# Sixteen gate tiles computed in the front's seven-product pairs instead of in the mixer steps

## The reference, cut to what matters

```python
u = rms_norm(x, norm_mix_pre_w)
proj = u @ w_in
z, xbc, dt_raw, q, k, v, gate_ssd, gate_attn = _split(proj, IN_SIZES)
xbc = jax.nn.silu(causal_dwconv(xbc, ssd_conv_w, ssd_conv_b))
...
y = gated_group_rms_norm(y.reshape(b, s, SSD_D_INNER).astype(x.dtype), z, ssd_norm_w)
y_ssd = y @ ssd_w_out
q = apply_rope(q.reshape(b, s, ATTN_N_KV_HEADS, ATTN_REP, ATTN_HEAD_DIM), cos, sin)
...
y_attn = sliding_window_sink_attention(q, k, v, attn_sinks) @ attn_w_out
merged = jax.nn.sigmoid(gate_ssd) * y_ssd + jax.nn.sigmoid(gate_attn) * y_attn
```

## Time and profile before

| | us |
|---|---|
| median of 3 runs | 2077.04 (2076.82 to 2079.41) |
| the profiled execution, its own time | 2077.58 |
| its span, first to last instruction | 2075.9 |
| PE busy | 2012.1 (97%) |
| DVE busy | 1339.8 (65%) |
| ACT busy | 968.4 (47%) |
| POOL busy | 603.2 (29%) |
| mean granted clock of TensorE | 0.991 |

### The profile page before, as it was taken

The page is one execution under the profiler, slowest core; times in us unless marked ns, Lnnn a source line. Parts: engine busy times, 40 slices in busy tenths (PEclk is TensorE's granted clock), DMA queues, the critical chain, the costliest instruction groups (busy, mean ns, idle before and its releaser), DMA issues. The chain is left out here.

```text
span 2075.9 us, 27004 instructions
## 1 busy us (share of the span) xinstructions
PE 2012.1 (97%) x9612; PEld 1625.5 (78%) x9612; DVE 1339.8 (65%) x1812; ACT 968.4 (47%) x1815; POOL 603.2 (29%) x445
## 2 busy tenths in 40 slices
PE   6999999989999999999999999999999999999997
PEld 6777877867777777777678888888888888888886
DVE  6878787766666666666634445569877787753523
ACT  5633543535665565655633223335444444444432
POOL 6533234244444354444300000024222222100000
PEclk9999999999999999999999999999999999999999
DMA  4334244364443444433454333222212221455443
GB/s 157 91 112 142 92 134 151 100 203 139 129 139 120 139 143 129 139 109 113 151 200 167 124 145 142 105 80 82 91 66 86 91 89 62 165 175 184 121 147 91
DMA packets 168396, 262.00 MB, mean 126 GB/s; under 512 B 18656, under 2 KB 109152, under 8 KB 168288
## 3 DMA queue, kind: packets, MB, share of 16 engines
q1 hardware_dynamic: 129568, 208.15, 31.5%
q0 software_dynamic: 8368, 30.94, 4.4%
q10 hardware_dynamic: 30352, 21.50, 3.2%
HBM read 191.73 MB, written 63.57 MB: 123 GB/s over the span
## 5 line engine op out<-in xcount | busy, mean ns | idle before, releaser
L2792 DVE TENSOR_TENSOR lt_d_lo<-lt_w_raw,lt_d_hi 128x640 fp32r<-128x640 f32 (+1 forms) x62 | 55.3, 892 | 133.4 <-ACT lt_d_hi L2491 133.3
L1538 POOL TENSOR_TENSOR mx_seg<-mx_seg,mx_cbm 128x1024 f32<-128x1024 f32 x31 | 75.2, 2426 | 168.4 <-ACT mx_seg L1635 168.4
L162 PE MATMUL ps_zg<-u_hi,g_hi 128*128 128x512 f32 x256 | 109.8, 429 | 1.9 <-DVE g_lo L1212 1.9
L162 PE MATMUL ps_zg<-z_w,u_hi 128*128 128x512 f32 x256 | 103.9, 406 | 3.6 <-DVE z_w L1714 3.6
L2362 POOL TENSOR_TENSOR lt_t_f<-lt_w_raw 128x512 f32<-128x512 f32 x21 | 29.1, 1387 | 261.7 <-DVE lt_t_lo L2720 260.2
L2491 ACT ACTIVATE lt_d_hi<-lt_w_raw 128x640 fp32r<-128x640 f32 (+1 forms) x62 | 49.1, 792 | 118.6 <-PE lt_ps L164 102.9
L164 PE MATMUL ps_zg<-u_hi,g_lo 128*128 128x512 f32 x256 | 102.2, 399 | 0.0
L163 PE MATMUL ps_zg<-u_lo,g_hi 128*128 128x512 f32 x256 | 101.8, 398 | 0.0
L164 PE MATMUL ps_zg<-z_w,u_lo 128*128 128x512 f32 x256 | 100.3, 392 | 0.0
L163 PE MATMUL ps_zg<-z_w,u_hi 128*128 128x512 f32 x256 | 99.8, 390 | 0.0
L2449 ACT ACTIVATE lt_t_hi<-lt_t_f 128x512 fp32r<-128x512 f32 x84 | 52.4, 628 | 100.1 <-PE lt_ps L164 61.9
(11 more groups left out here) (553 smaller groups left out, 6612.1 us busy)
## 6 DMA issues: line engine op xcount, KB each, us to landing
lt_w_raw<-in_w_up SPq DMA_DIRECT2D x44, 512.0 KB, 4.5
work<-acs_s SPq DMA_DIRECT2D x32, 512.0 KB, 4.2
lt_sig<-gate_s SPq DMA_DIRECT2D x24, 512.0 KB, 3.5
lt_w_raw<-in_w_down SPq DMA_DIRECT2D x32, 384.0 KB, 3.2
ff_s<-lt_fo SPq DMA_DIRECT2D x21, 512.0 KB, 5.4
tok_s<-fr_xt SPq DMA_DIRECT2D x20, 512.0 KB, 3.2
lt_w_raw<-in_w_down SPq DMA_DIRECT2D x32, 320.0 KB, 3.0
g_raw<-in_w_gate SPq DMA_DIRECT2D x16, 512.0 KB, 6.7
```

What stands on the lines that cost most here:

```text
L162: pe.matmul(dst, s_hi, m_hi, start=first, stop=False, skip_group_check=onto)
L1538: pool.tensor_tensor(seg[:], (carry.a_row[:, 0] if opening else seg[:]), cbm[:].unsqueeze(1).to_broadcast([P, HPG, P]), ALU.mult).then_inc ...
L2792: dve.tensor_tensor(down_w(m)[1][:, 0:n], w_raw[:, m % 2, 0:n], down_w(m)[0][:, 0:n].bitcast(F32), ALU.subtract).then_inc(dw_lo_done, 1)
```

## The change

The gate product leaves the mixers. `ORDER` gets eight pairs of kind "g", spread among the others, and the front computes the 16 gate tiles as such pairs: seven block products each, two plain copies to `xc` on ACT and a store of each by SP (`store_gate`). The last pair is now a gate pair, so that the front no longer ends with a convolution and a silu. In the mixers the gate products, the splits of their weights (ACT, DVE), the copy of the result, its DMA and the loads of gate weights are gone. The weights of the attention's output, which used the gate's place, are loaded at c = 4 of the last group by SP. Both banks of `ps_zg` now hold z in turn. z of the next step is cut in two: k from 0 to 3 (`AHEAD = 4`) after the turned outputs, the rest where it stood; z of the next group's first step stays whole behind the diagonal products. The table work of the front (dt, sums) moves to the iterations after gate and rotary pairs. Slots 1 and 2 of PSUM change places.

In numbers of instructions PE loses 768 matmuls of the mixers and gains 672 in the front. ACT and DVE lose 16 splits of 1024 elements and ACT loses 32 copies; in the front they gain 56 splits each of 512 elements, ACT 8 copies of a partial product and 16 of tiles (128 by 1024), DVE 40 additions of 512 elements, and POOL 32 sums of weights.

The diff, cut to its core:

```diff
-ORDER = (("c", 0), ("c", 1), ("r", 0), ("c", 8), ("r", 4), ("c", 10), ("c", 2), ("c", 3), ("r", 1), ("c", 4), ("c", 9),
-         ("r", 2), ("c", 5), ("c", 6), ("c", 7), ("r", 3), ("c", 11))
+ORDER = (("c", 0), ("c", 1), ("g", 0), ("r", 0), ("c", 8), ("g", 1), ("r", 4), ("c", 10), ("g", 2), ("c", 2), ("c", 3),
+         ("r", 1), ("g", 3), ("c", 4), ("c", 9), ("r", 2), ("g", 4), ("c", 5), ("c", 6), ("g", 5), ("c", 7), ("g", 6),
+         ("c", 11), ("r", 3), ("g", 7))
...
+            def store_gate(n):
+                t = tiles[n]
+                sp.wait_ge(kept, t.kept_n + 1)
+                sem = carry.g_late if t.i == LAST else g_stored[t.j]
+                sp.dma_start(gate_s[t.f], xc[:, t.j]).then_inc(sem, 16)
...
             taken(2 * i)
             high_z(6)
             high_z(7)
-            act.wait_ge(carry.g_in[0], 16)
-            act.wait_ge(product_done, OPS * (i - 1) + 5)
-            act.activation(carry.g_hi[:, 0], carry.g_raw[:, 0], ACT.Copy).then_inc(carry.g_hi_done, 1)
             taken(2 * i + 1)
-            silu(2 * i)
-            silu(2 * i + 1)
...
-                if i == 2:
+                if i == 3:
                     table_dt_first()
-                if i == 4:
+                if i == 6:
                     table_dt_rest()
...
             last.then_inc(carry.z_done, 1)
-            pe.wait_ge(carry.g_lo_done, 1)
-            for k in range(4):
-                matmul3(pe, carry.ps[:, 1], carry.g_hi[:, 0, k], carry.g_lo[:, 0, k], u_hi[:, k, 0:HALF],
-                        u_lo[:, k, 0:HALF], k == 0, False)
+            for k in range(AHEAD):
+                matmul3(pe, carry.ps[:, 1], u_hi[:, k, P:2 * P], u_lo[:, k, P:2 * P], carry.z_hi[:, k], carry.z_lo[:, k],
+                        k == 0, False)
...
+            def z(g, c, ks):
+                n = NT * g + c
+                if ks[0] == 0 and n >= 2:
+                    pe.wait_ge(z_used, n - 1)
...
+                    def ahead(*ks):
+                        if c < NT - 1:
+                            z(g, c + 1, range(*ks))
+
                     if not opening:
-                        gate(g, c, range(0, 4), opening)
                         values(*before)
...
-                    gate(g, c, range(4, 6), opening)
...
                     if not opening:
                         turn_outputs(*before, first and c == 1)
-                    gate(g, c, range(6, KT), opening)
+                    if not opening:
+                        ahead(0, AHEAD)
...
-                    next_z(g, c, last_group, range(KT))
+                    ahead(AHEAD, KT)
+                    if c == NT - 1 and not last_group:
+                        z(g + 1, 0, range(KT))
```

More of the change, by code:

```diff
@@ L31 @@
 TH = NT // 2
+AHEAD = 4
 KH = KT // 2
@@ L407, in xc_free @@
             before = tiles[n - 2]
-            if not before.conv:
+            if before.rot:
                 eng.wait_ge(q_stored[before.j], 16 * (before.q_n + 1))
+            if before.gate:
+                eng.wait_ge(g_stored[before.j], 16 * (before.gate_n + 1))
             if before.turns:
@@ L419, in xt_free @@
                 return
-            before = next((t for t in reversed(tiles[:n]) if t.j == n % 2 and (t.turns or not t.conv)), None)
+            before = next((t for t in reversed(tiles[:n]) if t.j == n % 2 and (t.turns or t.rot)), None)
             if before.conv:
@@ L1457, in group @@
                 for c in range(NT):
-                    if c % 2 == 0:
-                        u = 4 * g + c // 2
-                        if not (last and c == NT - 2):
-                            src = A["w_attn_out"][0] if last and c == NT - 4 else A["w_gate"][u + 2]
-                            sp.wait_ge(g_lo_done, u + 1)
-                            sp.dma_start(g_raw[:, (c // 2) % 2], src).then_inc(g_in[(c // 2) % 2], 16)
+                    if last and c == NT - 4:
+                        for j in range(2):
+                            sp.dma_start(g_raw[:, j], A["w_attn_out"][j]).then_inc(out_in[j], 16)
                     if last and c == NT - 1:
@@ L1657, in group @@
                         split_o(0)
-                    if change:
-                        gate_tile(g, c, first)
                     if change:
@@ L1668, in group @@
                     ins.then_inc(exp_done, 1)
-                    if not change:
-                        gate_tile(g, c, first, ending)
-                    if last and c == NT - 3:
-                        act.wait_ge(g_lo_done, 2 * KT)
-                        act.dma_start(g_raw[:, 1], A["w_attn_out"][1]).then_inc(g_in[1], 16)
                     if not (last and c == NT - 1):
@@ L1705, in _ @@
             outputs(NG - 1, NT - 1, False, False)
-            for j in range(2):
-                act.wait_ge(g_stored[j], 16 * NG * NT // 2)
         @block.vector
```

187 lines of the change are left out of this document (69 added, 118 removed).

## The result

The changed kernel takes 2127.03 us (median of 4, 2126.54 to 2128.89) where the kernel before takes 2076.93: a ratio of 1.0242, 95% interval 1.0225 to 1.026, so 50 us slower. The forecast was 2111, the range 2090 to 2142. The profiled execution has a span of 2124.8 us for 2075.9 before, 48.9 us more.

What follows compares the result with a forecast made beforehand. The kernel was taken as bound by matmuls on PE, the changed mixers by latency over ACT and DVE. 152.3 - 12 - 96 - 10.5 = +33.8 us on 2077.58 gave 2111 us, range 2090 to 2142.

Steps and rivals of the forecast that it cites:

- Term 1: Front: eight added gate pairs of 19.04 us each cost PE +152.3 us; their work on other engines is covered.
- term 2: Front: about half of PE's stalls in the pairs go, -12 us (between -5 and -20).
- Term 3: Mixers' steps: the ACT and DVE chain sets them, 15.2 us a middle step; -96 us (between -85 and -106).
- Rival C: Mixers' steps: the clock falls once a step, +50 us, so about 2160 us; chance 0.06.
- Rival B: Mixers' steps stay bound by PE because the chain holds slack; 12.7 us a step, kernel 2034 us; chance 0.06.
- Term 4: Joint of front and mixers: earlier mixer start and lighter first step, together -10.5 us (between -7 and -13).
- rival D: Mixers: POOL's blocking or loads put a middle step at 16 to 16.5 us, +25 us, 2136 us; chance 0.10.

Runs made afterwards that it cites:

- e9_loads: The changed kernel with only SP's loads of the step after next issued some 4.5 us sooner: 2131.11 us.
- e5_tail: The changed kernel with the last 6 of a step's 24 z products behind its transposes of the scores: 2122.99 us.
- e3_mask_first: The changed kernel with DVE's mask and maximum ahead of its product with z in all steps but the last: 2121.15 us.
- e2_z_behind: The changed kernel with all of z behind the diagonal products in every step: 2264.90 us.
- e7_all: e6_mask_tail plus DVE's SBUF sum for y before its wait for the diagonal products, 6 next-group z products earlier at c = 7, ACT's output-weight splits later: 2087.38 us.
- e6_mask_tail: The changed kernel with the edits of e3_mask_first and e5_tail together: 2107.44 us.

## Why the prediction was right, and where its terms were off

**Term 1 and term 2, the front.** +152.3 - 12 = +140.3 was forecast, +141.3 came. The last product of the pairs ends at about 573.7 us for the 572 forecast. The waits fell by 9.2 us, from 17.8 to 8.6; the first one, 3.6 us, stayed as said. By an estimate from the granted clock, its lower level cost 6.8 us in the pairs before (0.57 over 99 to 107 us, 0.66 over 126 to 131 and 174 to 179) and costs 5.2 now (0.57 over 100 to 108 and over 240 to 244), 1.6 less. Together 10.8 us went where I took 12, and 152.3 - 10.8 = 141.5 is close to the measured 141.3. The pair's price of 19.04 us was right, and the run with two gate pairs confirms that nothing beside matmuls is paid.

**Term 3, the mixers.** -96 was forecast, -84.7 came, and this is where the forecast lost 11.3 of the 15 us that its sum is short. Middle steps (15.17 for 15.2), c = 0 (13.1 for 13.1), the waits for the copy (1.11 for 1.1) and the product with z (+6.77 for +6.78) came as worked out. The misses by step: c = 7 took 21.08, 19.89 and 21.01 for 18.3 each, +7.1 us in three; the last two 16.72 and 16.71 for 15.2 and 15.3, +2.9; c = 1 14.75 to 15.26 for 14.7, +1.3 in four, of which the late loads are the part that e9_loads takes away (14.75 in all four). That is the +11.3 between 472 and 483.2. The step of the working that failed is the one on c = 7. I noted that the whole z stays behind the diagonal products there, and counted the splits on DVE and POOL, but did not ask what then covers ACT's copy of the turned outputs, which I had found to be covered by little in a middle step. Before, all 24 gate matmuls of a step stood ahead of the product with the state, the last 6 of them right over this copy. With them gone and no z in their place it is a wait of 2.89 us, and the clock falls at its end. The run with the filler puts the step at 18.5, so 6.4 of the 7.1 us are this wait and its clock.

**Rival C** had 0.06. As told, a fall in every step, it did not come: the granted clock over the mixers is 0.96, and 1.00 in the middle steps. But its mechanism is what made c = 7 long, at 3.5 us a fall and not the 1.6 that I took from the front, and in the run with all of z behind it came in each step and cost more than the +50 I gave it: of the 140.0 us by which the mixers are longer there, the waits for ACT's copy make 83 at most (26 of 2.89 us and two of 3.83). In the middle steps an empty wait of 1.1 us was followed by no fall, and one of 2.89 us by a fall in most steps. The Trainium skill, page "TensorE: Matmul & The Clock Gate", section "A second HAM failure mode: psum-queue depth-cycling", lets short idle gaps between groups of matmuls make the clock oscillate; the middle steps, with a gap of 1.1 us in each, speak against that for gaps of this size, the run with gaps of 2.89 us agrees with it.

**The ground of the middle step.** I had it bound by the chain over ACT and DVE alone, with PE keeping up. That chain does set the step, as e5_tail shows, but the others stand close behind it. The runs show three rounds, of 15.17 (ACT and DVE), 14.8 (PE with its empty wait for the copy) and 14.2 us (DVE's sums for y). Rival B's condition, that the chain holds slack, could not have given B's 2034: behind the chain stood PE at 14.8, above B's break-even of 14.1; with that edit the mean over all 31 steps is 473.4 / 31 = 15.3.

**Term 4, the joint.** -10.5 was forecast, -8.3 came. The mixers' first work on ACT starts 10.6 us behind the first z (584.16 us) for 16.4 before, -5.8 for the -6.5 forecast; from there to the first copy it is -2.5 for -4. **`late`**: 0 forecast, +0.5 came.

**The sum.** 141.3 - 8.3 - 84.7 + 0.5 = +48.8 where I had +33.8. All terms erred the same way, so no miss hid another. But the 31 us that the range left above 2111 were meant for a slower chain (rival D), and the steps c = 7 and the end, which I had not foreseen, fell into them: in that the range was lucky. The reason given, that the gate products filled waits that are still there, is what the last kernel bears out from the other side: with every round opened the mixers take 431.2 us, 136.7 less than before, and the first copy comes 133.3 us later (597.33 against 464.02). So the change breaks even only when almost every wait that the gates covered has found another cover.

## What to carry to other kernels

Before you take work from the engine that is busiest, write down for each wait of the step, in the odd steps too (first, last, the one that changes weights), what lies over it now and what will lie over it then. When a step becomes a matter of latency, look for all rounds that close at about its length; one edit then shows nothing, and two or three together do. When a wait goes, ask who was held back by it and whom it will run into.

## What the runs showed of the hardware

The clock's fall is not the same each time. With one and the same wait of 2.89 us PE's clock stayed at 1.00 in one step of e3_mask_first and fell in two others (0.52 over 813 to 823 us), which cost 3.5 us each; in e2_z_behind one step paid 3.7 to 4.3 us beyond the wait and the next 1.1 to 1.7, by the two lengths above. The length of a single wait does not decide it either. The waits of 1.54 us in every middle step of e5_tail were followed by no fall (1.00 granted over 656 to 672 us), and one of 1.58 in e7_all was:

```profile
699.66 0.85 PE L1853 MATMUL mx_ps_e<-ident,raw_pieces 128*128 128x128 f32 x4 [1.58 <-DVE raw_pieces L1789]
```

```profile
700.00:703.00 3.00, 3.00 (x10) 2.42 (x9) 2.09 (x5) 1.97 (x4) 2.38 (x1) 0.50 0.88 241
```

DVE's operations on two SBUF operands of 128 by 512 took 0.66 us with POOL idle and 1.83 with POOL at work, while those with one operand in PSUM took 0.69 beside the same work; three splits took 3.35 or 5.05 us by POOL's start alone. The Trainium skill, page "SBUF — State Buffer", section "SBUF: two separate sides", calls the pair of ports that the two engines share "an **exclusive lock**, not a bandwidth split", for operations with two SBUF inputs against POOL's that read SBUF; the rows agree. POOL beside the slow sum of e6_mask_tail:

```profile
641.62 1.90 POOL L1511 TENSOR_TENSOR mx_seg<-work,acs 128x1024 f32<-128x1024 f32 x1 [3.27 <-PE mx_ps_d L1896]
```

The sum started at 642.24 us and ended at 644.07, 0.55 us after POOL's operation (643.52). Which of the two sums comes first was worth 0.5 us in each step here.
